# One inference step of a hybrid decoder: the memory rows at the beginning are transposed unscaled, their RMS scale is multiplied into the products, and the first weights are loaded tile by tile

## What is computed

```python
def rmsnorm(x, w=None):
    y = xf * lax.rsqrt(jnp.mean(xf * xf, axis=-1, keepdims=True) + EPS)
    if w is not None:
        y = y * w.astype(jnp.float32)

mn = rmsnorm(mem_prompt, norm_mem_w[l])
mk_p = (mn @ w_mem_k[l]).reshape(b, n_mem, MEM_HEADS, MEM_HD)   # 2048 x 512 weights
mv_p = (mn @ w_mem_v[l]).reshape(b, n_mem, MEM_HEADS, MEM_HD)   # 2048 x 512 weights
xn = rmsnorm(x, lp['norm_mix_w'])
z = xn @ lp['w_in']                                             # 2048 x 15872 weights
```

## Time and profile before

| | us |
|---|---|
| median of three runs | 3026.7 |
| the profiled execution | 3025.6 |
| its span, first to last instruction | 3023.8 |
| TensorE busy | 2956.2 (98%) |
| VectorE busy | 1820.0 (60%) |
| ScalarE busy | 1249.6 (41%) |
| GpSimd busy | 1026.4 (34%) |
| TensorE idle before its first instruction | 18.7 |

### The profile page before, as it was taken

How to read it: one execution, slowest core, us unless ns; L and a number is a source line. 1 busy time by engine, 2 the same in 40 slices (tenths; PEclk the granted TensorE clock), 3 DMA queues, 4 the chain that set the end, 5 groups by cost and what they waited for, 6 DMA issues and landing times.

```text
span 3023.8 us, 52241 instructions
## 1 busy us (share of the span) xinstructions
PE 2956.2 (98%) x20998; PEld 2765.3 (91%) x20998; DVE 1820.0 (60%) x2567; ACT 1249.6 (41%) x1382; POOL 1026.4 (34%) x550
## 2 busy tenths in 40 slices
PE   7999999999999999998999999999999999999998
PEld 6999999888999989998999999999999888888887
DVE  5444444465322156546388999877785677777664
ACT  5333322345543553333344534544454333333332
POOL 0000000134655520033088898777774011111000
PEclk9999999999999999999999999999999999999999
DMA  7555555476685756677588999999999788888773
GB/s 236 182 166 166 166 166 166 155 232 202 188 287 187 260 163 202 219 208 166 121 201 192 240 259 245 253 299 295 293 251 370 281 333 297 332 323 291 253 270 120
DMA packets 449327, 698.35 MB, mean 231 GB/s; under 512 B 31029, under 2 KB 345813, under 8 KB 421630
## 3 DMA queue, kind: packets, MB, share of 16 engines
q1 hardware_dynamic: 398526, 553.66, 59.5%
q10 hardware_dynamic: 41440, 75.68, 9.1%
q0 software_dynamic: 9216, 67.11, 6.0%
HBM read 629.24 MB, written 63.72 MB: 229 GB/s over the span
## 4 chain that ended last, share of the span: by engine, by line
PE 48%; DMA 1%; DVE 1%; ACT 0%; issue 0%; ACTq 0%; DVEq 0%
PE banks L2725 8%; PE banks L2723 8%; PE banks L2724 8%; PE banks L2656 7%; PE banks L2663 7%; PE banks L2657 7%; PE banks L2692 2%; DMA peer_area<-in_peer_u_dram 1%; PE banks L2676 0%; PE banks L2744 0%; DVE peer_keys_T_and_hot_rows L3022 0%; DVE peer_area L3079 0%; DVE peer_uT L2907 0%; ACTq L2560 0%; DVE peer_area L2898 0%
## 5 line engine op out<-in xcount | busy, mean ns | idle before, releaser
L2756 POOL TENSOR_TENSOR peer_uT_low<-peer_uT,peer_uT_high 128x1024 fp32r<-128x1024 f32 x256 | 615.7, 2428 | 247.9 <-ACT peer_uT_high L2783 247.3
L1107 POOL TENSOR_TENSOR gate_low<-gate_raw,gate_high 128x512 fp32r<-128x512 f32 x192 | 256.2, 1350 | 824.7 <-ACT gate_high L1062 807.1
L2656 PE MATMUL banks<-x_high,peer_uT_high 128*128 128x256 f32 x2048 | 493.1, 283 | 0.0
L2657 PE MATMUL banks<-x_low,peer_uT_high 128*128 128x256 f32 x2048 | 489.0, 280 | 0.0
L2656 PEld LDWEIGHTS banks<-x_high,peer_uT_high 128*128 128x128 f32 x2048 | 386.6, 189 | 0.2
L2657 PEld LDWEIGHTS banks<-x_low,peer_uT_high 128*128 128x128 f32 x2048 | 385.8, 188 | 0.0
L279 PE MATMUL banks<-x_high,win_high 128*128 128x288 f32 (+1 forms) x1312 | 349.4, 296 | 0.0
L280 PE MATMUL banks<-x_low,win_high 128*128 128x288 f32 (+1 forms) x1312 | 348.7, 295 | 0.0
L249 ACT ACTIVATE win_high<-win_raw 128x2048 fp32r<-128x2048 f32 x84 | 160.8, 1915 | 332.7 <-DVEq L241 320.0
L2783 ACT ACTIVATE peer_uT_high<-peer_uT 128x1024 fp32r<-128x1024 f32 x256 | 260.9, 1054 | 57.1 <-DVE peer_uT L2907 56.7
L2907 DVE STREAM_TRANSPOSE peer_uT<-peer_u 128x1024 f32<-128x1024 f32 x192 | 234.3, 1230 | 79.1 <-DMA peer_u<-in_peer_u_dram 55.9
(11 more groups left out here) (408 smaller groups left out, 6306.8 us busy)
## 6 DMA issues: line engine op xcount, KB each, us to landing
win_raw<-in_w_in_dram SPq DMA_DIRECT2D x38, 2048.0 KB, 8.1
peer_u<-in_peer_v_dram SPq DMA_DIRECT2D x64, 1024.0 KB, 5.1
peer_area<-in_peer_v_dram SPq DMA_DIRECT2D x64, 1024.0 KB, 5.1
gate_raw<-in_w_in_dram SPq DMA_DIRECT2D x96, 512.0 KB, 5.7
peer_u<-in_peer_u_dram ACTq DMA_DIRECT2D x192, 256.0 KB, 6.7
peer_u<-in_peer_u_dram SPq DMA_DIRECT2D x192, 256.0 KB, 5.9
w_raw<-in_w_up_ret_dram SPq DMA_DIRECT2D x8, 2048.0 KB, 8.9
w_raw<-in_w_out_dram SPq DMA_DIRECT2D x8, 2048.0 KB, 8.7
```

The lines of the kernel that those rows point to most:

```text
L1107: pool.tensor_tensor(self.low[:, p % 2, c, :, :], self.raw[:, p % 4, :, c * P:(c + 1) * P], self.high[:, p % 2, c, :, :], ALU.subtract).th ...
L2656: pe.matmul(out, UH[:, c, k, :], XH[:, k, 0:DENSE], start=(k == 0), stop=False)
L2657: pe.matmul(out, UH[:, c, k, :], XL[:, k, 0:DENSE], start=False, stop=False)
L2756: pool.tensor_tensor(UL[:, m % 2, part, :], UT[:, m % 2, part, :], UH[:, m % 2, part, :], ALU.subtract).then_inc(low, 1)
```

## The change

The memory rows are transposed as they were loaded. Their sums of squares are made later, on ScalarE, behind the high parts of units 0 and 1; VectorE makes the reciprocal roots behind the evacuation of unit 1 and writes them on the diagonal of two 128 x 128 matrices; after unit 2 TensorE multiplies these by the matrix of ones, which spreads the scale over all partitions as one row of 256 tokens (bank 7). Units 0 and 1 are evacuated unscaled and multiplied by the row in place afterwards; units 2 to 7 are multiplied by it as they are evacuated. The first buffer of weights comes in two loads of 128 columns (runs of 512 bytes). The identity and the memory's gain are issued by ScalarE's queue, the gain of x behind the x rows. The low part of unit 0 is made by GpSimd. ScalarE makes the high part of unit 0 between the eighth and the ninth tile of the memory.

```diff
@@ sync
                 for t in range(2):
                     sp.dma_start(mem_rows[:, t, :], mem[t * P:(t + 1) * P]).then_inc(mem_loaded[t], 16)
-                sp.dma_start(ident[:], C["ident"]).then_inc(ident_loaded, 16)
-                with nc.allow_non_contiguous_dma(reason="one gain per partition"):
-                    sp.dma_start(mem_gain[:], A["norm_mem_w"][0].rearrange("(k p) -> p k", p=P)).then_inc(gains_loaded, 16)
-                    sp.dma_start(x_gain[:], A["norm_mix_w"][0].rearrange("(k p) -> p k", p=P)).then_inc(gains_loaded, 16)
-                for b in range(2):
-                    w.load(sp, 0, b, [w_mem[0][:, :, b * 2 * P:(b + 1) * 2 * P]], first=True)
+                for u, landed in enumerate((w.loaded[0], second_loaded)):
+                    sp.dma_start(w.raw[0][:, :, u * P:(u + 1) * P], w_mem[0][:, :, u * P:(u + 1) * P]).then_inc(landed, 16)
+                w.load(sp, 0, 1, [w_mem[0][:, :, 2 * P:4 * P]], first=True)
                 for t, (_, r) in enumerate(TOKEN_TILES):
                     sp.dma_start(x_rows[0:r, t, :], x_in[t]).then_inc(x_loaded[t], 16)
+                with nc.allow_non_contiguous_dma(reason="one gain per partition"):
+                    sp.dma_start(x_gain[:], A["norm_mix_w"][0].rearrange("(k p) -> p k", p=P)).then_inc(x_gain_loaded, 16)
                 diff.load(sp)
@@ scalar
+                act.dma_start(ident[:], C["ident"]).then_inc(ident_loaded, 16)
+                with nc.allow_non_contiguous_dma(reason="one gain per partition"):
+                    act.dma_start(mem_gain[:], A["norm_mem_w"][0].rearrange("(k p) -> p k", p=P)).then_inc(mem_gain_loaded, 16)
                 act.wait_ge(constants_set, after(2))
+                act.wait_ge(mem_gain_loaded, after(16))
+                for k in range(KT):
+                    if k == KT // 2:
+                        w.split_high(act, 0, 0)
+                    act.wait_ge(turned, after(k + 1))
+                    act.activation(XH[:, k, 0:MEM_TOKENS], PS[:, 2 + k % 6, 0:MEM_TOKENS], ACT.Copy,
+                                   scale=mem_gain[:, k:k + 1]).then_inc(mem_high, 1)
+                act.wait_ge(second_loaded, after(16))
+                w.split_high(act, 0, 1)
                 for t in range(2):
                     act.wait_ge(mem_loaded[t], after(16))
                     square(mem_rows[:, t, :], P, t)
                 act.wait_ge(mem_steps, after(1))
                 act.activation(root[:, 0:2], ms[:, 0:2], ACT.Sqrt).then_inc(mem_steps, 1)
-                w.split_high(act, 0, 0)
-                act.wait_ge(gains_loaded, after(32))
-                for k in range(KT):
-                    ...
-                w.split_high(act, 0, 1)
@@ gpsimd
                 G["signals"].start_rest(pool)
+                w.split_low(pool, 0, 0)
@@ tensor
-                pe.wait_ge(mem_scaled, after(2))
+                for t in range(2):
+                    pe.wait_ge(mem_loaded[t], after(16))
@@
+                    if n == 2:
+                        pe.wait_ge(constants_set, after(2))
+                        pe.wait_ge(rstd_spread, after(2))
+                        for t in range(2):
+                            last = pe.matmul(PS[:, 7, t * P:(t + 1) * P], ones[:], diagonal[:, t, :], start=True, stop=True)
+                        last.then_inc(rstd_spread, 1)
@@ vector
+                def spread_rstd():
+                    roots_inverted(slice(0, 2), mem_steps)
+                    dve.wait_ge(mem_steps, after(6))
+                    for t in range(2):
+                        dve.tensor_scalar(diagonal[:, t, :], ident[:], rstd[:, t:t + 1], float(P), ALU.mult, ALU.mult).then_inc(rstd_spread, 1)
@@ keep_mem
-                    dve.tensor_copy(out[:, u, :], PS[:, u % 2, 0:MEM_TOKENS]).then_inc(w.bank_free, 1)
+                    if (i, u) < (0, 2):
+                        dve.tensor_copy(out[:, u, :], PS[:, u % 2, 0:MEM_TOKENS]).then_inc(w.bank_free, 1)
+                        if u == 0:
+                            dve.wait_ge(squared, after(2))
+                            mean_squares(slice(0, 2), mem_steps)
+                        else:
+                            spread_rstd()
+                    else:
+                        if (i, u) == (0, 2):
+                            dve.wait_ge(rstd_spread, after(3))
+                            dve.tensor_copy(rstd_row, PS[:, 7, 0:MEM_TOKENS]).then_inc(rstd_spread, 1)
+                            dve.wait_ge(rstd_spread, after(4))
+                        dve.tensor_tensor(out[:, u, :], PS[:, u % 2, 0:MEM_TOKENS], rstd_row, ALU.mult).then_inc(w.bank_free, 1)
+                        if (i, u) == (0, 2):
+                            dve.wait_ge(w.bank_free, after(2 + 2))
+                            dve.tensor_tensor(out[:, 0:2, :], out[:, 0:2, :], rstd_row.unsqueeze(1).to_broadcast([P, 2, MEM_TOKENS]),
+                                              ALU.mult).then_inc(rstd_spread, 1)
+                            dve.wait_ge(rstd_spread, after(5))
@@ body of the vector program
-                dve.wait_ge(squared, after(2))
-                rstds(slice(0, 2), mem_steps)
-                dve.wait_ge(mem_steps, after(6))
-                for t in range(2):
-                    dve.tensor_scalar(mem_rows[:, t, :], mem_rows[:, t, :], rstd[:, t:t + 1], None, ALU.mult).then_inc(mem_scaled, 1)
-                dve.wait_ge(gains_loaded, after(32))
+                dve.wait_ge(mem_gain_loaded, after(16))
                 for k in range(KT):
                     dve.wait_ge(mem_high, after(k + 1))
                     ...
-                w.split_low(dve, 0, 0)
+                dve.wait_ge(w.low_ready, after(1))
```

More of the change, by code:

```diff
@@ L783, in input_projections @@
         mem_rows = flat[:, 0:2 * D_MODEL].rearrange("p (i d) -> p i d", i=2)
-        (ident_loaded, constants_set, gains_loaded, squared, mem_steps, x_steps, mem_scaled, x_scaled_ready, turned, mem_high, mem_low,
+        diagonal = flat[:, 2 * D_MODEL:2 * D_MODEL + 2 * P].rearrange("p (i n) -> p i n", i=2)
+        rstd_row = flat[:, 2 * D_MODEL + 2 * P:2 * D_MODEL + 2 * P + MEM_TOKENS]
+        (ident_loaded, constants_set, mem_gain_loaded, x_gain_loaded, second_loaded, rstd_spread, squared, mem_steps, x_steps, x_scaled_ready, turned, mem_high, mem_low,
          xn_ready, x_high, x_low, raw_ready, spilled, projected, stored, tables_loaded) = st.sems(
-            "ident_loaded", "constants_set", "gains_loaded", "squared", "mem_steps", "x_steps", "mem_scaled", "x_scaled_ready",
+            "ident_loaded", "constants_set", "mem_gain_loaded", "x_gain_loaded", "second_loaded", "rstd_spread", "squared", "mem_steps", "x_steps", "x_scaled_ready",
             "turned", "mem_high", "mem_low", "xn_ready", "x_high", "x_low", "raw_ready", "spilled", "projected", "stored", "tables_loaded")
@@ L838, in square @@
                     act.wait_ge(squared, after(col))
-                    act.activation(PS[0:r, 2:6, :].rearrange("p b n -> p (b n)"), rows, ACT.Square,
+                    act.activation(x_scaled[0:r, col, :], rows, ACT.Square,
                                    accum_out=ss[0:r, col:col + 1]).then_inc(squared, 1)
@@ L960, in _, with mean_squares, roots_inverted @@
             def _(dve):
-                def rstds(cols, steps):
+                def mean_squares(cols, steps):
                     dve.tensor_scalar(ms[:, cols], ss[:, cols], 1.0 / D_MODEL, EPS, ALU.mult, ALU.add).then_inc(steps, 1)
+                def roots_inverted(cols, steps):
                     dve.wait_ge(steps, after(2))
@@ L978, in keep_mem @@
                         dve.wait_ge(squared, after(5))
-                        rstds(slice(2, 5), x_steps)
+                        mean_squares(slice(2, 5), x_steps)
+                        roots_inverted(slice(2, 5), x_steps)
                         diff.keep(dve)
@@ L982, in keep_mem @@
                         diff.weights(dve)
+                    if n == 5:
+                        dve.wait_ge(x_gain_loaded, after(16))
                     for k in {5: range(0, 6), 6: range(6, 12), 7: range(12, 16)}.get(n, ()):
```

3 lines of the change are left out of this document (removed).

## The result

The changed kernel takes 3037.1 us (median of six runs, 3035.4 to 3040.6) against 3026.7 (six runs too): ratio 1.0035, with an interval of 1.0024 to 1.0047. It is slower by 10.3 us, outside the predicted range of 3024 to 3033. The profiled execution has a span of 3034.3 us, 10.5 more than before.

The account below looks back on a forecast made before the run. TensorE, busy 2956.2 of 3023.8 us, was taken as the bound. Terms -1.6 + 0.8 + 2.1 + 1.15 + 0.06 = +2.5 us on 3025.6 gave 3028.1, as median 3029.2; range 3024.0 to 3033.0.

Parts of the forecast that it names:

- the shift D: Landing of the small loads that `diff.products` waits for: set by bytes, +0.8 us later, range -1.5 to +3.
- the new wait for room ahead of the gain of x moves that to about 32: SyncE's queue: last small load issued at about 32 instead of 28.78, still 4 us ahead of its landing.
- Rival 3: First weight loads: 512-byte packets cost as much as 1 KB ones, small loads land 5.5 us later, 3034.3 us; chance 0.09.
- TensorE could win 1.6 us ahead of `diff.products`: Before `diff.products`: an earlier start gains only 1.6 us while the small loads' landing stays.
- The stall and the half clock behind it: TensorE idles about 6.5 us ahead of `diff.products`, then runs at clock 0.50, losing 2.1 us.
- The chain behind unit 2: Spread row and scalings delay x's mean squares 1.7 us; unit 4, waiting for ScalarE's high part, starts 1.15 us later.
- The 0.06 us for evacuations with a multiplication: Units 4 to 7: evacuating with a multiplication takes 0.06 us more, one of them on the path, +0.06 us.
- The clock's rule: TensorE's gaps: 3.6 to 4.1 us idle drops the clock to 0.50, 2.0 us keeps 1.00.
- the row of the first transposes disagrees with a low clock at the start: Kernel start: first transposes, 0.23 us each at shown clock 1.00 after 18.7 idle us, contradict a low default clock.
- The start: Up to unit 1's end: first transpose at about 11, first product about 20 instead of 26.9, unit 1 ending 31 to 35.
- rival 1: Memory's gain lands near 16, unit 1 ends at 35, 3.2 us idle keeps the clock: 3027.1 us; chance 0.18.
- The move to GpSimd: Low part of unit 0 on GpSimd: at most 4.9 us, hidden behind TensorE's high products by 0.7 us.

Follow-up runs that it names:

- the run that kept the clock: Changed kernel with 70 idle products added on TensorE between unit 1 and `diff.products`: 3035.7 us against 3027.5 for the kernel before, ratio 1.0027.
- the changed kernel's second run: The changed kernel measured again with no edit, in a later series: 3036.8 us against 3028.5 for the kernel before, ratio 1.0029.
- its base: Changed kernel with the gain of x issued behind the fourteen small loads instead of ahead: 3026.3 us against 3027.5 for the kernel before, ratio 0.9996.

## Why the prediction was wrong

**The step that failed** is the shift D of the small loads' landing. I took +0.8 us, with +3 as the end of the range; it was +7.5. I worked it out from bytes, "set by bytes, not by progress". The trace of before allowed this, since there the DMA engines were busy from 13 to 34; but it also showed an issue of 5.52 us, and I used this row only as a clock for the rows' landing. I did ask what the queue would do ("the new wait for room ahead of the gain of x moves that to about 32"), and put the wait at the wrong entry. The gain itself is let in in 0.42 us; the entry behind it pays, and there it was 11.3 us long. With the last load issued at 39.3, and not at 32, the landing no longer hung on bytes. Moving the gain of x alone takes the shift away in the changed kernel (35.7) and brings 5.5 us of it in the kernel before (42.3). Rival 3 had a shift of this size, +5.5, and its time of 3034 was the nearest, but by a cause that the runs refute: packets of 512 bytes.

**Other terms of the sum**, by the same steps:

- TensorE could win 1.6 us ahead of `diff.products`: right. -1.6 + 7.5 = 5.9, and it started 5.87 us later.
- The stall and the half clock behind it: both there. 2.1 us were predicted; 2.1 is the difference between the changed kernel and the run that kept the clock. Unit 2 ended 7.98 us later, which is 5.87 + 2.1.
- The chain behind unit 2: +1.15 predicted, 60.77 - 54.31 = 6.46 us from the end of unit 2 to unit 4, against 5.49: +0.97. The mean squares of x came 2.0 us after the end of unit 2, 1.5 later than before (predicted 1.7), and the wait of TensorE was 0.4 us, not 0.7, its cause being ScalarE's high part as written.
- The 0.06 us for evacuations with a multiplication: nothing, the product takes 0.42 us like the copy.
- Not in the sum: behind the gap of 2.0 us ahead of w_in the clock fell, while before it had not the earlier trace rows. The first product with w_in took 7.9 us from its start to its end instead of 7.2, +0.8.

-1.6 + 7.5 + 2.1 + 1.0 + 0.8 makes 9.8 of the 10.5 us of the span. That is the whole shift at 110 us. Behind it the later gaps change it a little at a time: 9.6 us at the gap of 586.75, 9.2 at that of 1507.73, 10.5 from 2200 on.

**The clock's rule.** I took 2.0 us as a gap that keeps the clock and 3.6 as one that loses it. The trace of before has two more gaps of 2.0 us, ahead of 1380.76 and 2185.54, and both lose it. The second, as a row of TensorE's timeline and a stretch behind it:

```profile
2185.54 1.18 PE L2692 MATMUL banks<-peer_keys_T_and_hot_rows 128*128 128x128 f32 x8 [1.96 <-DVE peer_keys_T_and_hot_rows L3022]
```

```profile
2187.00:2188.00 1.00, 1.00 (x6) 1.00 (x6) 1.00 (x2) 0.73 (x1) 0.58 (x2) 0.50 1.05 440
```

The sentence that the row of the first transposes disagrees with a low clock at the start is wrong too: 0.23 us each is their pace at half clock, as the changed kernel's second run shows above. It changes no term of the sum.

**The start.** First transpose at 12.4 (predicted 11), first product at 24.3 (20), end of unit 1 at 35.9 ("between 31 and 35"). The rows took 7.1 us to landing instead of 6.1; the rest is the memory's gain, which landed at 16.7 as in rival 1, and the table load of 1.3 us, which I had named. Rival 1's cause was right, its consequence wasn't: the idle stretch was still 9 us. The move to GpSimd was sized well (at most 4.9, measured 4.61), and hidden by the 0.7 us that were stated. The estimate of 286 GB/s for runs of 512 bytes stands beside 292 measured. The Trainium skill (DMA: Bandwidth & Descriptors, Queues, rings and completion order) has an engine take turns between its queues by packet. The counts of packets bear that out (435 to 432, one for one), and the gain's landings fit it: 12.2 us on ScalarE's queue, 7.8 on SyncE's, and 14.5 on ScalarE's beside longer packets.

## What to carry to other kernels

A load with one small packet per value costs little where it stands and much where something urgent stands behind it: look at what follows it in the queue, and put it last or load it with fewer packets. When a start is brought forward, ask of the next waits in the order of work what sets their time, and if it is a transfer, take both its bytes and the time of its issue from the queue's timeline. An idle stretch won there can cost the clock: in the profile of the run with the memory's gain on SyncE's queue unit 1 ended 5.2 us earlier and unit 2 3.0 us later than in its base.

## What the runs showed of the hardware

- A queue entry behind 2048 packets of 4 bytes was held for 11.3 us, behind 1024 for 6.4, behind 128 packets of 64 bytes for none. In the first case the DMA engines were busy until 31 (share 1.08 from 28 to 29) and the hold ended at 33.1; the small loads behind it were then issued beside nearly idle engines (shares of 0.31 and 0.06 in the stretches shown).
- Behind the gap of 2.0 us ahead of w_in the granted clock fell to 0.50 in nine of the thirteen profiles, the changed kernel's two among them, and stayed at 1.00 in four: the kernel before, this kernel with the gain of x moved, and the runs with the idle products and with the tables' work behind later units. So the length of a gap alone did not decide in these runs.
- Two queues with work took turns one packet for one: 435 packets of 512 bytes against 432 of 4 bytes in one us, 287 of 1 KB against 283 of 4 bytes in another kernel. So 2048 packets of 4 bytes took 12.2 to 14.5 us to landing beside such a queue, and 7.8 us in the same queue behind the rows.
- The first transposes of an execution start 0.21 us apart, after 12.4 idle us as after 18.7 before, and this is their pace where the granted clock is 0.50. By the Trainium skill (TensorE: Matmul & The Clock Gate, Part 1) the low clock is the state from which work begins; these rows agree.
- How soon the clock was back at the beginning differed between runs that are the same up to there: the first products of unit 0 took 0.41 us each, up to 26.3, in the run with the gain of x behind the small loads, and 0.28 from the start in the run with the tables' work behind later units.
